# Who issues the stores of the up stage in a hybrid recurrent, attention and expert block on one core

## The chip, the cores and the metric

The kernel runs on one core of a Trainium2 chip. The metric is the device time of one execution in microseconds (us), as the median of several runs.

## The reference

The reference is one layer of a hybrid block over 1024 tokens of width 1024. A gated linear recurrence and a forgetting attention come first; neither is touched here. Behind them stands PEER: every token has 128 experts (8 heads of 16) out of 16384, each with one row of `u_tab` and one of `v_tab`. It is this part that the change is in:

```python
def block(args):
    xb, eb, gb = args
    pre = jnp.einsum('td,tkd->tk', xb.astype(jnp.float32), u_tab[eb].astype(jnp.float32))
    act = jax.nn.gelu(pre) * gb
    return jnp.einsum('tk,tkd->td', act, v_tab[eb].astype(jnp.float32))
```

`experts` (eb) come from two top-16 lists over 128 keys each, and `gates` (gb) are a softmax over the 16 picked scores of each head.

## The kernel before

The program is a row of stages, each a block in which the five engines run their own instruction lists and meet only through semaphores. The stages are: projection, recurrence, attention, output mix, scoring, `experts_up`, `experts_down`, and the last norm. The change is in `experts_up`, the up stage.

The up stage treats the tokens in two ways. The last 640 tokens are dense: for them `gelu(h @ u)` is computed for all 16384 experts, in NK = 128 chunks of 128 experts. The first 384 tokens go by rows: for each of the 384 slots (128 picks of 3 tiles) GpSimd gathers one u row for each of 128 tokens (`fetch`, an indirect DMA of 512 KB into a ring of 6 tiles `u_rows`), and VectorE forms the dot products (`dot`).

One dense chunk c goes through these steps. SyncE loads `u_chunk` (512 KB, two buffers) by `load(c)`. ScalarE copies it to `uT_hi` (`high`, L1559). VectorE subtracts to `uT_lo` (`low`, L1709; for the first 24 chunks GpSimd does it, L1612). TensorE multiplies 48 times into `expert_pre` (L1523), in two halves of 320 tokens, over four PSUM buffers. ScalarE applies the gelu into `expert_acts` (L1573, two buffers). SyncE stores `expert_acts` to `acts_dram` (320 KB, L1493).

Beside this the gates of the dense tokens are spread over the experts, in 160 groups of four tokens. VectorE makes one-hot rows (L1719, L1720), ScalarE multiplies them by the gates (`gate`, L1581 and L1584, eight small instructions for a group), TensorE multiplies them into `spread_ps` (L1513, L1515), and ScalarE copies the result into `pick_memory` (`spread_out`, L1566). When 8 groups are there, a part of 2 MB is stored to `gates_dram` (L1499); there are 20 such stores, one for about five chunks.

All engines walk a common numbering of quarters q, four for a chunk (QUARTERS = 512), and each engine's list is in the order of q. `high(c + 1)` stands at the start of chunk c, the two gelus at its second and fourth quarter. The order within SyncE's list is written out by hand: `load(c + 2)`, which waits for `low(c)`, then a wait for both gelus of chunk c and the store of them, then the gates store that may be due. A wait holds up everything behind it on the engine.

The semaphores that matter: `act_done` counts gelus, `act_stored` and `spread_stored` count stores landed (a gelu waits for the first before it writes a buffer again, `spread_out` for the second), `u_in` counts loads landed.

Of the kernel before, what the change touches and what calls it, by code (L numbers as in the profile page):

```python
# [1377 lines left out]
def experts_up(nc, d, m, sem):  # L1378
# [12 lines left out]
    GROUP, SLOTS, PART = 4, 4, 8  # L1391
# [4 lines left out]
    QUARTERS = 4 * NK  # L1396
# [6 lines left out]
    def paced(q, total, first, stop):  # L1403

        return min(max((q - first) * total // (stop - first), 0), total)

    groups_at = lambda q: range(paced(q, ALL, SPREAD_FROM, SPREAD_TO), paced(q + 1, ALL, SPREAD_FROM, SPREAD_TO))
# [22 lines left out]
    with ExitStack() as own_memory:  # L1430
# [5 lines left out]
        act_out = sb("expert_acts", [P, 2, DENSE])  # L1436
# [3 lines left out]
        spread = m.pick_memory[:, 0:2 * NK * 32].rearrange("p (b e t) -> p b e t", b=2, t=32)  # L1440
# [16 lines left out]
        pre_done, act_done = sem("pre_done"), sem("expert_act_done")  # L1457
        act_stored = [sem("act_stored0"), sem("act_stored1")]
        hot_done, gates_hot = sem("hot_done"), sem("gates_hot")
        spread_done, spread_read = sem("spread_done"), sem("spread_read")  # L1460
        spread_stored = [sem("spread_stored0"), sem("spread_stored1")]
# [10 lines left out]
        def wait_low(engine, c):  # L1472

            if c < POOL_LOWS:
                engine.wait_ge(ulo_pool, c + 1)
            else:
                engine.wait_ge(ulo_dve, c - POOL_LOWS + 1)

        with nc.Block() as block:
            @block.sync  # L1480
            def _(sp):
                def load(c):
                    if c >= 2:
                        wait_low(sp, c - 2)
                    sp.dma_start(u[:, c % 2], d.peer_u_turned[c]).then_inc(u_in[c % 2], 16)

                load(0)
                load(1)
                for c in range(NK):
                    if c + 2 < NK:  # L1490
                        load(c + 2)
                    sp.wait_ge(act_done, 2 * c + 2)
                    sp.dma_start(d.acts[c], act_out[:, c % 2]).then_inc(act_stored[c % 2], 16)  # L1493
                    for q in range(4 * c, 4 * c + 4):
                        for g in groups_at(q):
                            if (g + 1) % PART == 0:
                                part = g // PART
                                sp.wait_ge(spread_read, g + 1)
                                sp.dma_start(d.gates[part].rearrange("p e t -> p (e t)"),  # L1499
                                             spread[:, part % 2].rearrange("p e t -> p (e t)")  # L1500
                                             ).then_inc(spread_stored[part % 2], 16)
                for b in range(2):
                    sp.wait_ge(act_stored[b], 16 * (NK // 2))
                    sp.wait_ge(spread_stored[b], 16 * (ALL // PART // 2))
# [46 lines left out]
            @block.scalar  # L1551
            def _(act):
                A = nc.scalar.activation

                def high(c):
                    act.wait_ge(u_in[c % 2], 16 * (c // 2 + 1))
                    if c >= 2:
                        act.wait_ge(pre_done, 2 * c - 2)
                    A(uhi[:, c % 2], u[:, c % 2], ACT.Copy).then_inc(uhi_done, 1)  # L1559

                def spread_out(g):
                    part, col = divmod(g, PART)
                    act.wait_ge(spread_done, g + 1)
                    if col == 0 and part >= 2:
                        act.wait_ge(spread_stored[part % 2], 16 * (part // 2))
                    A(spread[:, part % 2, :, col * GROUP:(col + 1) * GROUP].rearrange("p e t -> p t e"),  # L1566
                      spread_ps[:, g % 2], ACT.Copy).then_inc(spread_read, 1)

                def gelu(c, half):
                    act.wait_ge(pre_done, 2 * c + half + 1)  # L1570
                    if half == 0 and c >= 2:
                        act.wait_ge(act_stored[c % 2], 16 * (c // 2))
                    A(act_out[:, c % 2, half * WIDTH:(half + 1) * WIDTH], pre[:, (2 * c + half) % 4, 0:WIDTH],  # L1573
                      ACT.Gelu_apprx_tanh).then_inc(act_done, 1)

                high(0)
                def gate(g):
                    t, first = g // GROUPS, g % GROUPS * GROUP
                    act.wait_ge(hot_done, g + 1)
                    for j in range(GROUP):  # L1580
                        A(second_lo[:, g % SLOTS, j], second_hi[:, g % SLOTS, j].bitcast(F32), ACT.Identity,  # L1581
                          scale=gate_lo[:, t % 2, first + j:first + j + 1])
                    for j in range(GROUP):
                        last = A(second_hi[:, g % SLOTS, j], second_hi[:, g % SLOTS, j].bitcast(F32), ACT.Identity,  # L1584
                                 scale=gate_hi[:, t % 2, first + j:first + j + 1].bitcast(F32))
                    last.then_inc(gates_hot, 1)

                for q in range(QUARTERS):
                    c = q // 4
                    if q % 4 == 0 and c + 1 < NK:  # L1590
                        high(c + 1)
                    if q % 2 == 1:
                        gelu(c, q % 4 // 2)
                    for g in groups_at(q):
                        spread_out(g)
                    for g in gates_at(q):
                        gate(g)
                    if q == KEYS_FROM - 4:
                        act.wait_ge(shifted, 1)
                        A(m.pair_val[:], below_top, ACT.Exp).then_inc(exp_done, 1)  # L1600
                    for f in range(F):
                        if q == min(dots_end[f] + 2, QUARTERS - 1):
                            act.wait_ge(dot_done, P * (f + 1))
                            A(dots[:, f], dots[:, f], ACT.Gelu_apprx_tanh).then_inc(dots_read, 1)

            @block.gpsimd
            def _(pool):
# [377 lines left out]
def hybrid_block(nc, args, stop=None):  # L1985
# [22 lines left out]
    with ExitStack() as memory:  # L2008
# [90 lines left out]
        with h2, picks:  # L2099
            with h2_rows_part:  # L2100
                score(nc, d, m, sem)
            if stop == "score": return m
            experts_up(nc, d, m, sem)
# [36 lines left out]
```

## Time and profile before

| What | Value |
|---|---|
| Runs | 2991.67, 2984.30, 2984.37 us; median 2984.37 |
| Profiled execution, first to last instruction (span) | 2987.8 us |
| Up stage, dense chunks | from 889.7 to 1988 us in the span |
| TensorE busy over the span | 2742.9 us (92%) |
| VectorE, ScalarE, GpSimd busy | 2346.0, 1253.3, 1435.8 us |
| Moved by DMA | 754.28 MB, mean 252 GB/s |

The profile gives no time of its own for what lies around the span. The span is 3.4 us over the median of the runs.

The profile names the engines PE (TensorE matmul), PEld (its weight load), DVE (VectorE), ACT (ScalarE), POOL (GpSimd) and SP (SyncE); SPq and ACTq are DMA issues on the queue of that engine. A row of a group names line, engine, operation and `out<-in` by the program's tile names. "Idle before" is the time for which the engine sat idle ahead of the instruction, and the arrow names what it waited for.

### The profile page before, as it was taken

Reading aid. Unit: us, or ns where it says so; the run is one execution under the profiler, and the core shown is the slowest. Engines: PE = TensorE matmul, PEld = TensorE weight load, DVE = VectorE, ACT = ScalarE, POOL = GpSimd, SP = SyncE. Lnnn points to the kernel's source line nnn. Section 1 sums busy time; section 2 is a strip of 40 time slices with the busy share of each in tenths; the row PEclk is TensorE's granted clock in tenths of the full one; section 3 lists DMA queues with packets and bytes.
Section 4 is the critical chain, followed back from the end, with each engine's and each line's share of the span. In section 5 each row is a group of like instructions: output and inputs, shape, how many; then the busy total and the mean of one; then the engine's idle time right before and its main releaser. Section 6 shows DMA issues by size and latency. Waiting matters only on the chain. (4 is left out here: it accounts for less than half of the span.)

```text
span 2987.8 us, 40185 instructions
## 1 busy us (share of the span) xinstructions
PE 2742.9 (92%) x15003; PEld 2397.9 (80%) x15003; DVE 2346.0 (79%) x4170; ACT 1253.3 (42%) x2507; POOL 1435.8 (48%) x1107
## 2 busy tenths in 40 slices
PE   7998799989989999999999999954999999999996
PEld 6776576459989999999999999953887787787875
DVE  3375786327968888997898988747999999999997
ACT  3244333112223277777778788722222222222222
POOL 1111210004745765555455555534666666667663
PEclk9999799989999999999999999986999999999998
DMA  4110100211103799999899999989999999999996
GB/s 117 36 42 14 57 1 22 84 58 42 37 29 119 268 330 328 355 346 326 325 355 347 339 370 362 356 314 344 375 382 362 380 383 366 382 383 372 385 375 226
DMA packets 315442, 754.28 MB, mean 252 GB/s; under 512 B 22944, under 2 KB 141728, under 8 KB 312688
## 3 DMA queue, kind: packets, MB, share of 16 engines
q0 software_dynamic: 111104, 403.02, 36.4%
q1 hardware_dynamic: 203088, 344.50, 32.6%
q10 hardware_dynamic: 1056, 4.19, 0.3%
q8 instruction: 119, 1.95, 0.3%
q14 instruction: 75, 0.61, 0.1%
HBM read 659.35 MB, written 92.27 MB: 252 GB/s over the span
## 5 line engine op out<-in xcount | busy, mean ns | idle before, releaser
L1829 POOL DMA_INDIRECT v_rows<-in_peer_v,row_numbers x384 | 614.6, 1601 | 370.8 <-DVE y L1893 242.1
L1621 POOL DMA_INDIRECT u_rows<-in_peer_u,row_numbers x384 | 535.7, 1395 | 421.1 <-DVE row_weights L1726 367.5
L1523 PE MATMUL expert_pre<-h2T,uT_hi 128*128 128x320 f32 x4096 | 674.4, 313 | 43.7 <-DVE uT_lo L1709 27.6
L1523 PEld LDWEIGHTS expert_pre<-h2T,uT_hi 128*128 128x128 f32 x4096 | 614.7, 190 | 51.5 <-DVE uT_lo L1709 32.7
L1935 PE MATMUL expert_out<-v_hi,w_hi 128*128 128x512 f32 x1280 | 503.5, 393 | 91.1 <-DVE w_lo L1872 91.0
L1893 DVE SCALAR_TENSOR_TENSOR y<-v_rows,row_weights,y 128x1024 f32<-128x1024 f32 x384 | 489.1, 1282 | 62.6 <-DMA v_rows<-in_peer_v,row_numbers 45.5
L1935 PE MATMUL expert_out<-v_lo,w_hi 128*128 128x512 f32 x1280 | 501.5, 392 | 0.0
L1935 PE MATMUL expert_out<-v_hi,w_lo 128*128 128x512 f32 x1280 | 500.9, 391 | 0.0
L1726 DVE CUSTOM_DVE_ANT_0 u_rows<-u_rows,h_rows_kept 128x1024 f32<-128x1024 f32 x384 | 468.8, 1248 | 17.2 <-DMA u_rows<-in_peer_u,row_numbers 17.2
L1935 PEld LDWEIGHTS expert_out<-v_hi,w_hi 128*128 128x128 f32 x1280 | 242.1, 189 | 149.7 <-DVE w_lo L1872 99.6
L1853 ACT ACTIVATE w_hi<-acts_times_gates 128x640 fp32r<-128x640 f32 x128 | 94.8, 741 | 626.9 <-DVE acts_times_gates L1865 626.9
L1523 PE MATMUL expert_pre<-h2T,uT_lo 128*128 128x320 f32 x2048 | 343.5, 309 | 0.0
L1523 PEld LDWEIGHTS expert_pre<-h2T,uT_lo 128*128 128x128 f32 x2048 | 313.3, 189 | 0.0
L1935 PEld LDWEIGHTS expert_out<-v_hi,w_lo 128*128 128x128 f32 x1280 | 242.3, 189 | 50.9
L1935 PEld LDWEIGHTS expert_out<-v_lo,w_hi 128*128 128x128 f32 x1280 | 242.0, 189 | 49.9
L1581 ACT ACTIVATE second_hot_lo<-second_hot_hi,gateT_lo 128x128 fp32r<-128x128 f32 x640 | 203.5, 393 | 64.3 <-DVE second_hot_hi L1720 64.1
L1709 DVE TENSOR_TENSOR uT_lo<-u_chunk,uT_hi 128x1024 fp32r<-128x1024 f32 x104 | 127.2, 1223 | 123.6 <-ACT uT_hi L1559 122.7
L1584 ACT ACTIVATE second_hot_hi<-second_hot_hi,gateT_hi 128x128 fp32r<-128x128 f32 x640 | 203.4, 392 | 0.0
L1566 ACT ACTIVATE pick_memory<-spread_ps 128x512 f32<-128x512 f32 x160 | 178.8, 1118 | 18.1 <-PE spread_ps L1515 18.0
L1573 ACT ACTIVATE expert_acts<-expert_pre 128x320 f32<-128x320 f32 x256 | 112.4, 439 | 161.6 <-PE expert_pre L1523 160.9
L1559 ACT ACTIVATE uT_hi<-u_chunk 128x1024 fp32r<-128x1024 f32 x128 | 135.6, 1060 | 101.6 <-DMA u_chunk<-in_peer_u_turned 101.6
L1851 ACT ACTIVATE v_hi<-v_chunk 128x1024 fp32r<-128x1024 f32 x128 | 134.5, 1051 | 95.7 <-PE expert_out L1935 78.0
(300 smaller groups left out, 4188.8 us busy)
## 6 DMA issues: line engine op xcount, KB each, us to landing
u_chunk<-in_peer_u_turned SPq DMA_DIRECT2D x128, 512.0 KB, 6.9
v_chunk<-in_peer_v SPq DMA_DIRECT2D x128, 512.0 KB, 9.6
acts_dram<-expert_acts SPq DMA_DIRECT2D x128, 320.0 KB, 4.9
gates_dram<-pick_memory SPq DMA_DIRECT2D x20, 2048.0 KB, 11.0
acts_times_gates<-acts_dram SPq DMA_DIRECT2D x128, 320.0 KB, 10.5
gates_group<-gates_dram SPq DMA_DIRECT2D x32, 1280.0 KB, 18.5
w_in_columns<-in_w_in SPq DMA_DIRECT2D x20, 512.0 KB, 4.0
wq_tile<-in_peer_wq SPq DMA_DIRECT2D x16, 512.0 KB, 4.0
```

What stands on the lines that cost most here:

```text
L1523: last = nc.tensor.matmul(pre[:, (2 * c + half) % 4, 0:WIDTH], part[:, c % 2, k], m.h2T[:, t, k, HALVES[half]], start=n == 0, stop=n == le ...
L1559: A(uhi[:, c % 2], u[:, c % 2], ACT.Copy).then_inc(uhi_done, 1)
L1566: A(spread[:, part % 2, :, col * GROUP:(col + 1) * GROUP].rearrange("p e t -> p t e"), spread_ps[:, g % 2], ACT.Copy).then_inc(spread_read, 1)
L1581: A(second_lo[:, g % SLOTS, j], second_hi[:, g % SLOTS, j].bitcast(F32), ACT.Identity, scale=gate_lo[:, t % 2, first + j:first + j + 1])
L1584: last = A(second_hi[:, g % SLOTS, j], second_hi[:, g % SLOTS, j].bitcast(F32), ACT.Identity, scale=gate_hi[:, t % 2, first + j:first + j ...
L1621: pool.indirect_dma_start(rows[:, k % RING], None, d.peer_u, bass.IndirectOffsetOnAxis(ap=m.row_of[:, f, slot:slot + 1], axis=0)).then_inc ...
L1709: v.tensor_tensor(ulo[:, c % 2], u[:, c % 2], uhi[:, c % 2].bitcast(F32), ALU.subtract).then_inc(ulo_dve, 1)
L1726: v.tensor_tensor_reduce(out=rows[:, k % RING], in0=rows[:, k % RING], in1=m.h2_kept[:, f], scale=1.0, scalar=0.0, op0=ALU.mult, op1=ALU.a ...
L1829: pool.indirect_dma_start(rows[:, k % ROW_RING], None, d.peer_v, bass.IndirectOffsetOnAxis(ap=m.row_of[:, f, slot:slot + 1], axis=0)).then ...
L1851: nc.scalar.activation(vhi[:, n % 2, c], vt[:, x % V_RING], ACT.Copy).then_inc(vhi_done, 1)
L1893: v.scalar_tensor_tensor(out=m.y[:, f], in0=rows[:, k % ROW_RING], scalar=m.row_weight[:, f, slot:slot + 1], in1=m.y[:, f], op0=ALU.mult, ...
L1935: last = nc.tensor.matmul(out[:, bank], a[:, n % 2, c, tokens], e[:, n % 2, c, cols], start=opens and k == 0, stop=closes and k == len(ter ...
```

## The change

ScalarE now issues the stores of activations and gates in the up stage; SyncE's list keeps the loads of u, and at its end the waits for the last stores. `store_acts(c - 1)` stands behind `high(c + 1)` at the start of chunk c, `store_gates` at the start of the quarter that follows the spreading of a part's last group. The data moved and the semaphores are the same.

```diff
                 for c in range(NK):
                     if c + 2 < NK:
                         load(c + 2)
-                    sp.wait_ge(act_done, 2 * c + 2)
-                    sp.dma_start(d.acts[c], act_out[:, c % 2]).then_inc(act_stored[c % 2], 16)
-                    for q in range(4 * c, 4 * c + 4):
-                        for g in groups_at(q):
-                            if (g + 1) % PART == 0:
-                                part = g // PART
-                                sp.wait_ge(spread_read, g + 1)
-                                sp.dma_start(d.gates[part].rearrange("p e t -> p (e t)"),
-                                             spread[:, part % 2].rearrange("p e t -> p (e t)")
-                                             ).then_inc(spread_stored[part % 2], 16)
...
+                def store_acts(c):
+                    act.wait_ge(act_done, 2 * c + 2)
+                    act.dma_start(d.acts[c], act_out[:, c % 2]).then_inc(act_stored[c % 2], 16)
+
+                def store_gates(part):
+                    act.wait_ge(spread_read, PART * (part + 1))
+                    act.dma_start(d.gates[part].rearrange("p e t -> p (e t)"),
+                                  spread[:, part % 2].rearrange("p e t -> p (e t)")
+                                  ).then_inc(spread_stored[part % 2], 16)
+
                 for q in range(QUARTERS):
                     c = q // 4
                     if q % 4 == 0 and c + 1 < NK:
                         high(c + 1)
+                    if q % 4 == 0 and c:
+                        store_acts(c - 1)
+                    for g in groups_at(q - 1) if q else []:
+                        if (g + 1) % PART == 0:
+                            store_gates(g // PART)
                     if q % 2 == 1:
                         gelu(c, q % 4 // 2)
...
+                    if q == QUARTERS - 1:
+                        store_acts(c)
```

In the lists below, names in square brackets are the semaphores that an instruction waits for. This is SyncE's list before the change, around the first gates store, with the load that follows it:

```order
L1485 DMA u_chunk<-in_peer_u_turned 128x1024 [waits u_lo_by_dve]
L1493 DMA acts_dram<-expert_acts 128x640 [waits expert_act_done]
L1499 DMA gates_dram<-pick_memory 128x4096 [waits spread_read]
L1485 DMA u_chunk<-in_peer_u_turned 128x1024 [waits u_lo_by_dve]
L1493 DMA acts_dram<-expert_acts 128x640 [waits expert_act_done]
```

And this is the whole of SyncE's list of the up stage with the change, up to the branch that ends the stage:

```order
L1480 UNCONDITIONAL_BRANCH [waits barrier_Pool_Activation_PE_DVE_SP_release]
L1485 DMA u_chunk<-in_peer_u_turned 128x1024 x2
L1485 DMA u_chunk<-in_peer_u_turned 128x1024 [waits u_lo_by_pool] x24
L1485 DMA u_chunk<-in_peer_u_turned 128x1024 [waits u_lo_by_dve] x102
L1479 UNCONDITIONAL_BRANCH [waits act_stored1,spread_stored1,spread_stored0,act_stored0]
```

Each load now waits for a subtraction alone; no store and no wait for a gelu stands between two loads.

ScalarE's list before, at the place in the program that corresponds to the first gates store:

```order
L1584 ACTIVATE second_hot_hi<-second_hot_hi,gateT_hi 128x128 x4
L1559 ACTIVATE uT_hi<-u_chunk 128x1024 [waits pre_done,u_in1]
L1566 ACTIVATE pick_memory<-spread_ps 128x4x128 [waits spread_done]
L1573 ACTIVATE expert_acts<-expert_pre 128x320 [waits act_stored0,pre_done]
L1581 ACTIVATE second_hot_lo<-second_hot_hi,gateT_lo 128x128 [waits hot_done]
```

The same place with the change, where a line of ScalarE has a number lower by ten:

```order
L1574 ACTIVATE second_hot_hi<-second_hot_hi,gateT_hi 128x128 x4
L1549 ACTIVATE uT_hi<-u_chunk 128x1024 [waits pre_done,u_in1]
L1580 DMA acts_dram<-expert_acts 128x640 [waits expert_act_done]
L1556 ACTIVATE pick_memory<-spread_ps 128x4x128 [waits spread_done]
L1584 DMA gates_dram<-pick_memory 128x4096 [waits spread_read]
L1563 ACTIVATE expert_acts<-expert_pre 128x320 [waits act_stored0,pre_done]
L1571 ACTIVATE second_hot_lo<-second_hot_hi,gateT_lo 128x128 [waits hot_done]
```

ScalarE has 148 DMA issues more, 128 of activations and 20 of gates. The store of activations stands right behind the copy to `uT_hi`; 15 of the 20 gates stores stand right behind a `spread_out`, the other five behind a store of activations.

## Rows read from the trace of the kernel before

**Rows 1.** The page: busy time of each engine over the span.

```profile
PE 2742.9 (92%) x15003; PEld 2397.9 (80%) x15003; DVE 2346.0 (79%) x4170; ACT 1253.3 (42%) x2507; POOL 1435.8 (48%) x1107
```

**Rows 2.** Stretches: length, busy us of PE, PEld, DVE, ACT, POOL, granted clock, DMA share, GB/s.

```profile
998.00:1063.00 65.00, 58.70 (x392) 56.86 (x393) 49.58 (x69) 23.35 (x52) 57.80 (x36) 1.00 0.91 321
1063.00:1988.00 925.00, 896.88 (x6329) 891.08 (x6327) 793.13 (x1187) 703.12 (x1730) 491.01 (x354) 0.99 0.92 343
1736.00:1871.00 135.00, 134.58 (x964) 134.28 (x964) 112.80 (x178) 110.34 (x273) 77.18 (x56) 1.00 0.96 364
```

**Rows 3.** Who waited for whom, 1063 to 1988 us: total us, times, longest.

```profile
DVE uT_lo L1709 <- ACT uT_hi L1559: 122.7, 40, 8.2
ACT uT_hi L1559 <- DMA u_chunk<-in_peer_u_turned: 97.1, 23, 7.4
ACT second_hot_lo L1581 <- DVE second_hot_hi L1720: 64.1, 45, 3.4
ACT expert_acts L1573 <- PE expert_pre L1523: 42.0, 43, 3.1
PE expert_pre L1523 <- DVE uT_lo L1709: 27.6, 21, 4.0
DVE u_rows L1726 <- DMA u_rows<-in_peer_u,row_numbers: 1.8, 2, 1.0
```

**Rows 4.** The same stretch, waits of SyncE's queue.

```profile
SPq L1493 <- ACT expert_acts L1573: 813.6, 105, 15.6
```

**Rows 5.** Timeline of SyncE's queue, ScalarE and VectorE from 1734 us: start, duration, instruction.

```profile
1738.09 1.23 DVE L1709 TENSOR_TENSOR uT_lo<-u_chunk,uT_hi 128x1024 fp32r<-128x1024 f32 x1 [1.36 <-ACT uT_hi L1559]
1743.72 0.43 SPq L1499 DMA_DIRECT2D gates_dram<-pick_memory  x1
1744.20 0.47 SPq L1485 DMA_DIRECT2D u_chunk<-in_peer_u_turned  x1
1757.48 1.06 ACT L1559 ACTIVATE uT_hi<-u_chunk 128x1024 fp32r<-128x1024 f32 x1 [4.01 <-DMA u_chunk<-in_peer_u_turned]
```

**Rows 6.** Timeline of TensorE: four of its 21 waits for `uT_lo`, first and last among them.

```profile
1163.94 4.63 PE L1523 MATMUL expert_pre<-h2T,uT_hi 128*128 128x320 f32 x16 [4.00 <-DVE uT_lo L1709]
1342.05 3.43 PE L1523 MATMUL expert_pre<-h2T,uT_hi 128*128 128x320 f32 x16 [2.62 <-DVE uT_lo L1709]
1577.31 2.03 PE L1523 MATMUL expert_pre<-h2T,uT_hi 128*128 128x320 f32 x12 [2.14 <-DVE uT_lo L1709]
1973.17 2.62 PE L1523 MATMUL expert_pre<-h2T,uT_hi 128*128 128x320 f32 x16 [3.17 <-DVE uT_lo L1709]
```

**Rows 7.** Stretches behind four of TensorE's waits, columns as in Rows 2.

```profile
1161.50:1172.00 10.50, 8.06 (x39) 8.06 (x39) 9.34 (x15) 9.15 (x23) 3.62 (x3) 0.67 0.76 274
1342.00:1347.00 5.00, 4.95 (x23) 4.96 (x24) 5.00 (x9) 5.00 (x14) 2.39 (x2) 0.66 0.85 262
1396.00:1401.00 5.00, 4.12 (x19) 4.13 (x20) 5.00 (x8) 5.00 (x16) 1.56 (x2) 0.72 0.33 60
1486.00:1491.00 5.00, 4.75 (x22) 4.76 (x23) 5.00 (x7) 1.59 (x6) 0.00 (x0) 0.66 0.35 143
```

**Rows 8.** DMA issues over the whole span: engine, count, KB each, median us to landing.

```profile
u_chunk<-in_peer_u_turned SPq DMA_DIRECT2D x128, 512.0 KB, 6.9
gates_dram<-pick_memory SPq DMA_DIRECT2D x20, 2048.0 KB, 11.0
u_rows<-in_peer_u,row_numbers POOLq DMA_INDIRECT x384, 7.3
```

**Rows 9.** Issues: ns min/median/max, first and last start; last row as in Rows 5.

```profile
L1485 SPq DMA_DIRECT2D u_chunk<-in_peer_u_turned x128: 327/433/2738, 882.2 to 1963.8; - x128
L1493 SPq DMA_DIRECT2D acts_dram<-expert_acts x128: 319/320/327, 899.0 to 1988.0; - x128
L1621 POOL DMA_INDIRECT u_rows<-in_peer_u,row_numbers x384: 932/1440/3046, 988.3 to 1966.1; - x192
1991.24 0.51 ACTq L1845 DMA_DIRECT2D y<-x_dram  x1
```

## The prediction

> **What bounds the kernel now.** I read the page first [rows 1]: TensorE is busy 92% of the span, no other engine over 79%, so time comes out of the kernel only where TensorE waits or runs at a low clock. Then the stretches of the stage that the change touches [rows 2]. The first 23 chunks end by about 1063 us. In the last part of them, from 998, TensorE idles 6.3 us while GpSimd, which does the subtractions there, is busy 57.8 of 65 us; no store is in that chain, and I expect nothing from it. The long stretch is 1063 to 1988 us, with 105 of the 128 chunks: 896.9 busy of 925, so 28.1 us idle.
>
> What would the stretch take if TensorE never waited? Between 1736 and 1871 us it is busy for 134.6 of 135 us at clock 1.00 and does 964 matmuls, 7.14 in a us. The 6329 matmuls of the long stretch take 886 us at that pace, 39 less than 925. That is the most that any change of the waits in this stretch can give: 28 us of idleness and some 10 in which it ran slower than full pace.
>
> The waits [rows 3] say what the idle time is: 27.6 us in 21 waits for `uT_lo` of VectorE. VectorE in turn waits 122.7 us for `uT_hi` of ScalarE, and ScalarE 97.1 us in 23 waits for the DMA of `u_chunk`. So a late load is the head of the chain. The timeline shows how one becomes late [rows 5]. At 1743.72 SyncE issues a gates store of 2 MB and at 1744.20, behind it in the same queue, a load of u. ScalarE gets the load only at 1757.48, 13.3 us after its issue, having sat idle for 4.0 us. The median load takes 6.9 us and a gates store 11.0 [rows 8].
>
> Why is the load behind the store at all? It reuses the buffer of a chunk whose `uT_lo` was finished at 1738.09 + 1.23 = 1739.3, so it could have gone 4.9 us earlier. SyncE was held by the wait for the gelus: that wait comes 105 times and takes 813.6 us, 7.7 us of every chunk [rows 4].
>
> **The change, part by part.**
>
> Loads without the stores in front. Each load is now issued when its subtraction is done, some 4 to 5 us sooner, in the example 4.4 us before the gates store instead of 0.5 us behind it. The next one goes during the store, but from another queue. A load needs 6.9 us typically, and the one in the example would have been wanted at 1753.5 (1757.48 less the 4.01 of idleness), 14.2 us after 1739.3: even the 13.3 us that it took behind the store would do. The longest of ScalarE's waits is 7.4 us; with a landing as slow as now and 4.9 us of lead, 2.5 would be left of it, and nothing of those under 4.9. I take the 97.1 us to fall below 10.
>
> What of that reaches TensorE. I followed each of its 21 waits back in the timeline; four of them are shown [rows 6]. Ten come directly behind a wait of ScalarE for the load: 19.9 us together, the first 4.00 and the last 3.17. Four more, 1.9 us, come in the one to four chunks after such a wait, while VectorE works off what piled up. The other seven, 5.8 us, have a VectorE that is late by its own work, like the 2.14 at 1577; these stay. So 21.8 us go.
>
> The clock. Behind four of the ten waits the granted clock is 0.67, 0.66, 0.72 and 0.66 [rows 7], a mix of its two levels 2.4 and 1.2 GHz; ahead of each TensorE had idled for 2.5 to 4 us. The cost is the missing share times the length: 3.5 + 1.7 + 1.4 + 1.7 = 8.3 us. It goes with the waits that it follows.
>
> 148 issues on ScalarE. On SyncE an issue takes 0.32 us for activations and 0.43 for gates; one on ScalarE's queue, in the next stage, 0.51 [rows 9]. In the long stretch that is 105 x 0.32 + 20 x 0.43 = 42 us more on ScalarE, 64 at 0.51 each. What can't overlap is a gates store: in 15 of 20 cases it waits for the `spread_out` just ahead to end, and ScalarE stands still for an issue. Its cover is the one to two chunks of lead with which `high` runs ahead of TensorE. I charge 5 us of new waits of TensorE; the bounds are 0 and the 42 us if no cover held.
>
> Longer reuse of buffers. A store of activations is issued behind `high(c + 1)`, some 2 to 3 us later than now, and can stand in the same queue behind a gates store of 11 us. The gelu that waits for it comes about one and a quarter chunks later, 11 us. A few gelus may wait a us or two; TensorE needs their PSUM buffer only two chunks on. Costed at nothing, inside the 5 us.
>
> Contention. The long stretch moves 343 GB/s x 925 us = 317 MB; in 886 us that is 358 GB/s. The stretch at full pace has 364 with the DMA engines 0.96 busy [rows 2]: near the edge, but it was run with TensorE never waiting. The gathers are a third party with 512 KB each, 384 of them in 978 us [rows 9], one in 2.55 us or 206 GB/s. While load, gates and gathers all run, a third of 364 GB/s would leave them 121, for the 4.3 us that a load takes at that rate: they fall behind by 0.37 MB, or 1.8 us. The ring of six tiles gives 6 x 2.55 = 15.3 us against a landing of 7.3 [rows 8], and VectorE waited only 1.8 us for gathers in the whole stretch [rows 3]. Costed at nothing.
>
> A rule of the Trainium skill speaks against the change: by its page "DMA: Bandwidth & Descriptors", section "Issuing engines are not separate DMA queues", transfers started by different engines run on the same 16 DMA engines and interleave, and several issuers save only issue time. By that rule alone the new queue itself brings nothing, and the rows do not dispute it; the gain would then be that of the earlier issue alone, which by the row of 4.9 us is nearly all of it.
>
> Sum: 21.8 + 8.3 - 5 = 25 us. The profiled span becomes 2987.8 - 25 = 2963; the span stands 3.4 us over the median run, so the median goes from 2984.4 to 2959.
>
> **The rivals.**
>
> The DMA engines are the bound. In that case a queue of its own only rearranges who waits: loads land early, and gates, activations or gathers late by as much. For it: the DMA share is 0.92 over the stretch and 0.96 at full pace. Against it: the 364 GB/s above. VectorE's `dot` would wait for gathers behind each of the 20 gates stores, 1.8 us each, 36 in all; if 21 of these reach TensorE by way of `uT_lo`, 4 us of gain are left: 2980.
>
> Half a gain. The stalls of ScalarE vanish, but VectorE, busy 793 of 925 us, or ScalarE, at full pace with its new issues at (110.3 + 6) of 135, take their place: 5.8 us of TensorE's waits are already of this kind. If they triple, that is 11.6 us more where I charged 5, and if half of the clock's 8.3 stays too, 11 of the 25 are lost: 2970.
>
> Slower, by ScalarE as an issuer. A DMA issue can be held up: on SyncE the longest took 2.74 us [rows 9]. On ScalarE everything stands behind it: `high`, then `uT_lo`, then TensorE. What is freed is 97 us; over 125 stores it is used up at 0.78 us each. From there ScalarE is busier than now, and at 1.6 us each it holds 703 + 200 = 903 us of work, over the 886 that TensorE needs; with a third of its remaining waits for VectorE and TensorE (64.1 + 42.0, so 35) it takes 938 us: 13 us slower, 2997. Against it: medians of 0.32 and 0.43, and a median is what counts over 125 of them.
>
> No effect at all would need that the load isn't held by SyncE's wait; the 813.6 us and the 4.9 us of the example exclude it.
>
> **How the numbers follow.** A measurement of this kernel tells a change from none at about 0.3%, 9 us, so faster is below 2975.4 and slower above 2993.3. My forecast, 2959, has 0.65, with its own range of 2950 (nothing charged to ScalarE, and 4 of the seven other waits' 5.8 us gone too) to 2969 (15 us charged). Half a gain has 0.15, most of it still faster; the DMA bound 0.12; the slower case 0.08. Faster is 0.65 + 0.12 = 0.77, same 0.15, slower 0.08. The range of 8 in 10 goes from 2949 to 2980: above it lie the slower case and half of the DMA case.
>
> **What would show it.** In the changed kernel's profile ScalarE's waits for `u_chunk` should be under 10 us, SyncE's queue should wait for `uT_lo` in every chunk, TensorE's waits for `uT_lo` of VectorE should be near 10 us instead of 27.6, the granted clock should be 1.00 in the stretch, and the up stage should end near 1963. The issues on ScalarE should last 0.3 to 0.5 us. I am wrong if `u_rows` appears as what VectorE waits for, if the landing of gathers rises over 10 us, if ScalarE's waits for its gates stores appear, or if the last stage takes the time back.

## The result: 2947.5 us, faster by 1.3%, just outside the range

The changed kernel takes 2947.52 us (median of 4 runs, 2946.64 to 2948.64). The kernel before, now with 4 runs, has a median of 2988.02 us (2984.30 to 2997.29); the fourth run, 2997.29, moved it up from the 2984.4 that the forecast started from. The ratio is 0.9869, with a 95% interval of 0.9844 to 0.9894. The prediction was 2959 us with a range from 2949 to 2980. The direction was right, and the gain is larger than forecast: 36.9 us below 2984.4, where 25 were forecast.

The page of the profile after, first line of busy times, answers to [rows 1]. The span is 2944.8 us against 2987.8.

```profile
PE 2728.3 (93%) x15003; PEld 2387.4 (81%) x15003; DVE 2348.3 (80%) x4170; ACT 1262.6 (43%) x2507; POOL 1431.7 (49%) x1107
```

To compare the up stage between kernels I measure it from the first matmul of `expert_pre` to the start of the last gelu, and split it where VectorE does its first `uT_lo` (chunk 24). The views by stretch give both parts: first the kernel before, then the changed one. Columns are as in [rows 2].

```profile
889.70:1067.80 178.10, 170.82 (x1146) 168.72 (x1147) 147.79 (x470) 58.13 (x109) 125.22 (x93) 0.99 0.60 203
1067.80:1987.60 919.80, 892.09 (x6295) 886.28 (x6293) 789.21 (x1183) 698.58 (x1721) 486.76 (x351) 0.99 0.92 344
```

```profile
890.20:1065.70 175.50, 171.94 (x1158) 170.63 (x1159) 146.64 (x462) 59.19 (x112) 121.05 (x94) 0.99 0.60 209
1065.70:1947.10 881.40, 878.65 (x6283) 877.02 (x6282) 790.63 (x1185) 706.38 (x1718) 487.92 (x351) 1.00 0.95 358
```

The later part shrank from 919.8 to 881.4 us, by 38.4. TensorE idled 27.7 us in it and now idles 2.75, and it is busy for 878.7 instead of 892.1 us. The two parts don't hold quite the same work: 12 matmuls more fall into the earlier part of the changed kernel (1158 against 1146) and 12 fewer into the later one, 1.7 us at the 7.14 matmuls in a us of the stretch at full pace. The earlier part gave 2.6 us, and what follows the up stage 2.5 (1000.2 to 997.7). With the start 0.5 us later, that is the 43.0 us between the two spans.

Who waited for whom in the later part of the changed kernel, beside [rows 3]:

```profile
ACT expert_acts L1563 <- PE expert_pre L1513: 73.1, 73, 3.1
DVE uT_lo L1716 <- ACT uT_hi L1549: 63.4, 35, 4.6
DVE u_rows L1733 <- DMA u_rows<-in_peer_u,row_numbers: 20.6, 18, 4.1
ACT expert_acts L1563 <- DMA acts_dram<-expert_acts: 3.7, 2, 2.7
PE expert_pre L1513 <- DVE uT_lo L1716: 2.7, 4, 2.1
```

ScalarE's wait for `u_chunk`, 97.1 us before, isn't in the list any more. TensorE's waits for VectorE went from 27.6 us in 21 to 2.7 in 4, where near 10 us had been forecast, and the stage ends at 1947 instead of the forecast 1963. VectorE's waits for gathers rose from 1.8 us to 20.6; the prediction had named this as a sign of being wrong.

SyncE's queue in the same stretch, beside [rows 4]: it now waits for the subtraction with each of its 102 loads, and for nothing else.

```profile
SPq L1485 <- DVE uT_lo L1716: 825.8, 102, 11.9
```

The timeline around one gates store shows the new order, beside [rows 5]: the subtraction ends at 1437.08 + 1.23 = 1438.31, the load is issued at 1438.34, and the gates store follows at 1438.84 on ScalarE's queue. The load landed 9.3 us later; the row of 1453.54, in which ScalarE takes it, has no wait.

```profile
1437.08 1.23 DVE L1716 TENSOR_TENSOR uT_lo<-u_chunk,uT_hi 128x1024 fp32r<-128x1024 f32 x1 [4.12 <-ACT uT_hi L1549]
1438.34 0.33 SPq L1485 DMA_DIRECT2D u_chunk<-in_peer_u_turned  x1
1438.84 0.33 ACTq L1584 DMA_DIRECT2D gates_dram<-pick_memory  x1
1444.55 0.33 ACTq L1580 DMA_DIRECT2D acts_dram<-expert_acts  x1
1453.54 1.04 ACT L1549 ACTIVATE uT_hi<-u_chunk 128x1024 fp32r<-128x1024 f32 x1
```

### The profile page after: what moved, and what is told of

Same layout as the page of the kernel before. It is cut to its first block and busy times, and to the rows that moved or that the text cites. A ratio compares the mean times of both kernels' runs of the same rounds, so it can differ in the third digit from the quotient of the medians.

```text
span 2944.8 us, 40185 instructions
## 1 busy us (share of the span) xinstructions
PE 2728.3 (93%) x15003; PEld 2387.4 (81%) x15003; DVE 2348.3 (80%) x4170; ACT 1262.6 (43%) x2507; POOL 1431.7 (49%) x1107
## 5 line engine op out<-in xcount | busy, mean ns | idle before, releaser
L1513 PE MATMUL expert_pre<-h2T,uT_hi 128*128 128x320 f32 x4096 | 667.3, 311 | 16.1 <-POOL uT_lo L1619 13.3
L1716 DVE TENSOR_TENSOR uT_lo<-u_chunk,uT_hi 128x1024 fp32r<-128x1024 f32 x104 | 127.2, 1223 | 64.2 <-ACT uT_hi L1549 63.4
L94 PE MATMUL product<-hT_hi_lo,w_in_hi 128*128 128x512 f32 x640 | 156.2, 396 | 3.4 <-DVE hT_hi_lo L223 2.4
```

Source lines behind the costliest of these rows:

```text
L94: last = nc.tensor.matmul(to, w[:, i % 2, k], m.hh[:, part, k, cols], start=n == 0, stop=n == len(terms) - 1)
L1513: last = nc.tensor.matmul(pre[:, (2 * c + half) % 4, 0:WIDTH], part[:, c % 2, k], m.h2T[:, t, k, HALVES[half]], start=n == 0, stop=n == le ...
L1716: v.tensor_tensor(ulo[:, c % 2], u[:, c % 2], uhi[:, c % 2].bitcast(F32), ALU.subtract).then_inc(ulo_dve, 1)
```

## The experiments

The change does two things to a load: it frees it from the wait for the gelus, and it takes the stores out of its queue. It also moves two kinds of stores and adds 148 issues to ScalarE. The first four kernels separate these.

**Stores on ScalarE, loads as late as before.** The changed kernel with one line more on SyncE:

```diff
                     if c + 2 < NK:
                         load(c + 2)
+                    sp.wait_ge(act_done, 2 * c + 2)
```

> The stores go on ScalarE's queue as in the change, but SyncE still waits for both gelus of chunk c before the next load, so the loads are issued as late as before the change. Theory A (the 2 MB gates store ahead of a load in the same queue makes that load late, and either a queue of its own or an earlier issue cures it): nearly the whole gain stays, 2950 to 2960 us, ScalarE waits under 25 us for u_chunk instead of 97. Rival B (the hold of 7.7 us a chunk is what costs): the gain is gone, 2980 to 2988 us. Rival C (the 16 DMA engines are shared, so a queue of its own brings nothing by itself): 2980 to 2988 us as well, with loads landing in 13 us behind each gates store.

The median is 2941.88 us, beside 2978.77 for the kernel before on the same chip, which the first four kernels share; the ratio is 0.9881 (0.9845 to 0.9916). The up stage took 1060.8 us. The loads behind the gates stores go nearly as late after their subtraction as before, 4.0 us by the median (4.9 before). ScalarE waited 19.2 us for `u_chunk`; the longest wait, 4.4, is for the first chunk of all, which every kernel has. In the later part:

```profile
ACT uT_hi L1550 <- DMA u_chunk<-in_peer_u_turned: 14.6, 11, 2.7
PE expert_pre L1514 <- DVE uT_lo L1717: 2.1, 1, 2.1
```

Theory A stands; B, that the hold in every chunk costs, falls. The loads don't land in 13 us either, as C had it. But this kernel changes two things, and not the queue alone. ScalarE issues a gates store sooner than SyncE did, so that the next load follows it by 0.8 to 7.4 us, 3.9 by the median; before, all 20 followed by 0.4 to 0.6 us. What the queue alone does is best seen where a load still goes close behind the store. In three profiles with all stores on ScalarE landing times can be read: the changed kernel's two and the last one of this section. There ten loads are issued 0.2 to 1.0 us behind a gates store, and they landed in 9.9 to 11.7 us. In the kernel before the 20 loads behind a gates store landed in 11.5 to 15.5, 13.4 by the median. So another queue, without the store of activations in it too, takes some 2.5 us off such a landing, an estimate from these two groups; at a greater distance the landings are shorter still (in the changed kernel's first profile 7.0 to 9.0 us for the twelve loads 4.5 to 9 us behind a store). How the gain of the stage splits between the two, no run shows.

**Loads early, all stores on SyncE.** Only SyncE's order is changed in the kernel before (`stores` holds its two waits and stores, unchanged):

```diff
                 for c in range(NK):
+                    if c >= 2:
+                        stores(c - 2)
                     if c + 2 < NK:
                         load(c + 2)
-                    sp.wait_ge(act_done, 2 * c + 2)
...
+                stores(NK - 2)
+                stores(NK - 1)
...
```

> All stores stay on SyncE and its queue, and nothing is added on ScalarE; only SyncE's order changes: the stores of chunk c - 2, then the load for c + 2, so that a load waits for its subtraction alone and goes some 4 us earlier, still behind the gates store in the queue. Theory A: a load of 13.3 us fits into the 14.2 us that it then has, so 2948 to 2955 us, as the change. Rival D (a queue of its own is what matters): 2975 to 2988 us, ScalarE still waits for the load behind each gates store.

The median is 2949.89 us, the ratio 0.9898 (0.9855 to 0.9940). The up stage took 1061.5 us, and ScalarE waited 4.5 us for `u_chunk`, in 2 waits, both for the first two chunks. In the later part TensorE's waits are gone too:

```profile
PE expert_pre L1529 <- DVE uT_lo L1715: 2.3, 2, 2.1
```

D falls: with the loads early a queue of their own isn't needed, and nor is ScalarE. Here too the new order moves the load away from the store: it follows 1.9 to 8.2 us behind it.

**Only the gates stores on ScalarE.** The kernel before without the gates stores on SyncE, and with `store_gates` of the change on ScalarE.

```diff
                     sp.dma_start(d.acts[c], act_out[:, c % 2]).then_inc(act_stored[c % 2], 16)
-                    for q in range(4 * c, 4 * c + 4):
...
+                    for g in groups_at(q - 1) if q else []:
+                        if (g + 1) % PART == 0:
+                            store_gates(g // PART)
...
```

> Only the 20 gates stores go to ScalarE; the stores of activations stay on SyncE, with the wait for the gelus between the loads. Theory A: 2950 to 2960 us, as with both moved but the loads late. Rival B (the hold in every chunk costs): 2980 to 2988 us.

The median is 2947.82 us, the ratio 0.9885 (0.9844 to 0.9925). The up stage took 1062.2 us. So 20 of the 148 moved stores are enough. The next load follows a gates store by 1.2 to 7.8 us here.

**Only the stores of activations on ScalarE.** The other half of the change:

```diff
                     if c + 2 < NK:
                         load(c + 2)
-                    sp.wait_ge(act_done, 2 * c + 2)
-                    sp.dma_start(d.acts[c], act_out[:, c % 2]).then_inc(act_stored[c % 2], 16)
...
+                    if q % 4 == 0 and c:
+                        store_acts(c - 1)
...
```

> Only the 128 stores of activations go to ScalarE; the gates stores stay on SyncE between the loads, each behind its wait for spread_out. In four of five chunks a load is free to go early, in the fifth it stands behind the gates store, late as before. Theory A: the late loads are exactly these, so hardly any gain, 2975 to 2988 us. Rival B: four fifths of the gain, 2955 us.

The median is 2949.53 us, the ratio 0.9916 (0.9883 to 0.9948). The up stage took 1071.1 us: 27 of the 41 us are won (21 of 34 by the second profile of the kernel before, see below), where I expected hardly any. Here theory A, in the form that I had given it, was wrong. These are the waits for the load and of TensorE in its later part, first in this kernel, then in the one with only the gates moved:

```profile
ACT uT_hi L1557 <- DMA u_chunk<-in_peer_u_turned: 38.4, 12, 8.0
PE expert_pre L1521 <- DVE uT_lo L1715: 9.2, 7, 3.8
```

```profile
ACT uT_hi L1551 <- DMA u_chunk<-in_peer_u_turned: 37.2, 20, 4.5
PE expert_pre L1515 <- DVE uT_lo L1710: 3.5, 7, 2.1
```

ScalarE waits for as long in both, 38 and 37 us, but TensorE loses 9.2 us in one and 3.5 in the other, and the later parts take 893.2 and 884.4 us. About 2 us of TensorE's waits, at chunk 80, are VectorE's own lateness in both; this wait stands in eleven of the twelve profiles. The rest differs by the long waits. Over the whole up stage the kernel before had ten waits of ScalarE over 5 us (7.38 the longest) and fifteen below; this one has two over 5 (8.02 and 6.09), and the one with the gates moved has none. In this kernel TensorE waits 3.83 us right behind the 8.02, and 2.10 right behind one of 4.76, but only 0.36 behind the 6.09.

In the two profiles of the kernel before, hardly any wait of ScalarE under 4 us is followed by one of TensorE within 4 us (one, by 0.36). The six between 4.0 and 4.9 behind the first chunk are followed by 0.42 to 2.31 us, or by nothing in one case, and those over 5 by anything from nothing to 4.0. So a single wait of up to 4 us costs TensorE next to nothing; above that the cost differs from chunk to chunk, and the length of the wait alone doesn't give it.

18 of the 20 loads are still issued 0.4 us behind a gates store here. But the loads behind a gates store go 0 to 5.4 us after their subtraction, 2.2 by the median, where it was 0.8 to 7.5 and 4.9 before, and that fits the fewer long waits. This is the nearest that the runs come to an earlier issue by itself.

**A swap on SyncE alone.** The kernel before, with a due gates store behind the next load instead of ahead of it; the loads still wait for the gelus.

```diff
+                load(2)
                 for c in range(NK):
-                    if c + 2 < NK:
-                        load(c + 2)
                     sp.wait_ge(act_done, 2 * c + 2)
                     sp.dma_start(d.acts[c], act_out[:, c % 2]).then_inc(act_stored[c % 2], 16)
+                    if c + 3 < NK:
+                        load(c + 3)
                     for q in range(4 * c, 4 * c + 4):
```

> The kernel before with one swap on SyncE: when a gates store is due, the next load is issued ahead of it instead of behind it. All stores stay on SyncE, and the loads still wait for the gelus. If only the load directly behind the 2 MB is too late, ScalarE's waits for u_chunk stay under 4.5 us each, and the up stage takes 1060 to 1064 us. If the next load, about 8 us later in the same queue, is as late, 1080 to 1098 us.

One run of 2953.55 us, beside 2982.72 of the kernel before on the same chip. The up stage took 1060.8 us, the same as with the stores on ScalarE and late loads. Its later part:

```profile
ACT uT_hi L1560 <- DMA u_chunk<-in_peer_u_turned: 25.0, 19, 3.4
PE expert_pre L1524 <- DVE uT_lo L1710: 2.1, 3, 1.7
```

The load that comes behind the store now follows it by 5.5 to 11.1 us. So the loss was in 20 places where a load stood right behind 2 MB in one queue, and the three cures of it are equally good, 1060.8 to 1061.5 us. The changed kernel is 3 to 5 us below them, about half of it in the earlier part. What they have in common is that no load is issued within 0.6 us behind a gates store in its own queue.

**What an issue costs ScalarE.** More issues behind `store_acts`, three or six in each chunk, of 8 KB each:

```diff
                 def store_acts(c):
                     act.wait_ge(act_done, 2 * c + 2)
+                    for j in range(3):
+                        act.dma_start(d.extra[c, j], m.ident[0:16]).then_inc(act_stored[c % 2], 16)
                     act.dma_start(d.acts[c], act_out[:, c % 2]).then_inc(act_stored[c % 2], 16)
```

> The changed kernel with three more DMA issues on ScalarE in each chunk (8 KB each, a constant into scratch memory, so nearly no bytes). An issue takes 0.33 us, so in the 105 later chunks this is 104 us more of ScalarE, which was idle for 175 of 881 us there, 41 of which its stores' issues took already. Theory A (the idle time of ScalarE covers issues): the up stage stays within 10 us of 1057. Rival E (each issue holds up the chain through high): 1160 us.

> The same with six more issues in each chunk, 208 us in the 105 later chunks, more than the 134 us that ScalarE has left. Theory A: the cover is used up, ScalarE becomes the bound and the up stage grows by at least 74 us, to 1131 or more. If issues run beside activations and cost ScalarE nothing, it stays at 1057. Rival E: 1265 us.

With three more the up stage took 1057.6 us, the same as the change. With six more it took 1108.9 us, 52 more than the change, and the one run 2997.42 us, slower than the kernel before with 2982.72 and 2978.38 in its runs on this chip. That is less than the bound of 74 that I gave. The extra issues, in the kernel with six:

```profile
L1581 ACTq DMA_DIRECT2D extra_dram<-ident x768: 308/442/1972, 896.8 to 1998.3; - x192
```

And its later part by stretch:

```profile
1063.70:1995.60 931.90, 901.14 (x6295) 889.90 (x6293) 791.45 (x1183) 695.53 (x1721) 475.01 (x351) 0.99 0.95 345
```

750 issues start on ScalarE in it. They last 393 us together, more than 0.44 us each, as many are longer than the median. Taken one by one from the timeline, 209 of the 393 us lie within an activation. The bound had left that out. In the changed kernel it is 35 of 40 us in 124 issues, and with three more in each chunk 167 of 225. Its waits show the way in which it reaches TensorE:

```profile
DVE uT_lo L1718 <- ACT uT_hi L1549: 107.9, 48, 7.0
ACT second_hot_lo L1571 <- issue: 68.9, 35, 6.9
...
PE spread_ps L1503 <- ACT second_hot_hi L1574: 16.7, 14, 4.8
```

The gates rows for the spreading are late, 16.7 us of TensorE, and `high` is too, by which VectorE waits 107.9 us where it was 63.4; of TensorE that is 10.7 us over the whole stage. So the way through `high`, which rival E named, is open here, but only once ScalarE is full. The cover is there, and it ends somewhere between four and seven issues a chunk; the change uses one, and a second in every fifth chunk.

**What repeats.** The kernel before and the changed one once more.

> The kernel before, unchanged, profiled a second time, to see what repeats. The up stage (first matmul of expert_pre to last gelu) took 1097.9 us in the first profile and 1056.9 with the change; I expect 1097 to 1099 again, with 25 to 30 us of TensorE's waits for uT_lo, while what follows the up stage, 1000.2 us before and 997.7 with the change, moves by several us without a cause in the program.

> The changed kernel, unchanged, profiled and timed a second time. The up stage should repeat at 1057 us within 2, TensorE's waits for VectorE's uT_lo under 4 us, and the ratio to the kernel before be 0.984 to 0.990.

The kernel before had an up stage of 1092.1 us (1097.9 in its first profile), 22.8 us of TensorE's waits for VectorE, and 997.7 us behind the stage. Both of the first two are below what I expected. The changed kernel had 1057.7 us (1056.9), 1.9 us of such waits, and the ratio 0.9878 (0.9849 to 0.9907): 2942.82 us, against 2979.55 for the kernel before on that chip. The gain repeats, though in the stage it is 34.4 us in this pair of profiles and 41.0 in the first: the kernel before varies by 5.8 us there, the changed one by 0.8. Over all twelve profiles the stage starts at 881.9 to 891.8 us, and what follows it takes from 984.0 to 1003.8, without any order in either. This is why whole times differ by 10 us where the stage of the changed kernel agrees within 1.

**The remaining waits.** The changed kernel with GpSimd's share of the subtractions cut:

```diff
-    POOL_LOWS = 24
+    POOL_LOWS = 14
```

> The changed kernel with GpSimd doing the subtraction for the first 14 chunks instead of 24, VectorE from there on. TensorE's last waits of any size in the up stage, 3.4 us in four, are for GpSimd, whose subtraction stands behind gathers from chunk 13 on; in the later chunks it is at full pace. If these four waits are all that is left, the up stage goes from 1056.9 to 1053 or 1054 us, which the time of the whole kernel can't tell from no change. Rival: VectorE, which does the key steps of the first tiles there, is late instead, 1057 to 1065 us.

The ratio is 0.9884 (0.9851 to 0.9916) and the up stage 1058.3 us. The waits for GpSimd after the first are gone, but those for VectorE rose to 6.2 us, 4.2 of it in chunk 14, where it takes over:

```profile
PE expert_pre L1513 <- DVE uT_lo L1716: 6.2, 3, 4.2
```

Nothing is gained; the changed kernel is not beaten by this one.

## Why the prediction was right in kind and too small in size

**Right: what bounded the stage, and the chain.** The head of the chain was the late load, and the late load was the one right behind the gates store. The eight profiles in which behind the first chunk no load makes ScalarE wait over 5 us, and ScalarE isn't overloaded, have an up stage of 1056.9 to 1062.2 us; the kernel before has 1092.1 and 1097.9. The forecast that ScalarE's waits for `u_chunk` fall below 10 us holds (5.4 us, all of it for the first two chunks), and so does the granted clock of 1.00.

**Right in the result, open in the share: the earlier issue.** The prediction set the rule of the Trainium skill's "DMA: Bandwidth & Descriptors", section "Issuing engines are not separate DMA queues", against the row of 4.9 us, and found that the earlier issue gives nearly all. Loads early in the same queue gave 1061.5 us. But stores on ScalarE with late loads gave 1060.8, 31 or 37 us less than the kernel before, by which of its profiles one takes. How much of that comes from the greater distance between store and load is open. By the rule several issuers save only issue time. The measurement differs: close behind a gates store a load landed in 9.9 to 11.7 us from another queue, and in 11.5 to 15.5 from the same. The same page's section "Queues, rings and completion order", by which each DMA engine takes turns between the queues that have work for it, agrees with this.

**Wrong: the sum.** The step that failed is "Sum: 21.8 + 8.3 - 5 = 25 us"; in the later part it was 38.4. All three of its terms were off in the same direction; counted for the same work, the 5 us charged for ScalarE are the largest error:

- The waits that go, 21.8 us: TensorE's waits for VectorE fell by 24.9 us in the stage's later part (27.6 to 2.7). I had kept seven waits, 5.8 us, as VectorE's own lateness. Only the one of 2.14 at 1577, in chunk 80, with a small one just ahead of it, has a counterpart (2.13 us in the changed kernel). The others were gone in every cured kernel, where 1.9 to 3.5 us remain in all, so I take them for late effects of the stalls. (The kernel with GpSimd's share cut has 6.2, but 4.2 of it in chunk 14, the first that VectorE takes over.) I had followed a stall for four chunks and stopped. In the second pair of profiles these waits fell by 20.9 us (22.8 to 1.9), so this term was off by no more than the kernel before varies.
- The slower pace, 8.3 us: TensorE's busy time in the later part fell by 13.4 us, 1.7 of it by the 12 matmuls fewer, so by 11.7 for the same work. In the second pair it fell by 11.8 (891.0 to 879.2), with 2 matmuls fewer. I had counted the four stretches in which the granted clock was seen low, and left out what was spread elsewhere. The first estimate, by the stretch at full pace, had 10.5, and 39 for both together; the measured 38.4 nearly reaches that ceiling. Where the 3.4 us beyond the 8.3 were lost isn't settled.
- The 5 us charged for ScalarE: nothing was lost. The 124 issues of the later part lasted 40 us, and 35 of these passed while an activation ran. One issue and even four a chunk are covered.

Beside the sum, 2.6 us came from the earlier part, where I expected nothing, or 4.3 with its 12 matmuls more. The changed kernel has 175.5 and 176.6 us there in its two profiles and 175.3 with three more issues a chunk; the kernel before has 178.1 and 178.0, and the first five experiments 177.8 to 178.9. What makes this is left open. The 2.5 us behind the stage are within its scatter.

**The rivals.** "The DMA engines are the bound" was half true and harmless: VectorE's waits for gathers rose to 20.6 us, and their landing from 7.3 us to 7.8 by the median, but neither reached TensorE; the stretch ran at 358 GB/s with a DMA share of 0.95, which is the 358 worked out. "Half a gain" didn't occur. "Slower, by ScalarE as an issuer" does exist, at six issues a chunk more, and its point is much further off than the 0.78 us a store that was given: four issues of 0.44 by the median, 1.8 us in a chunk, cost nothing.

**The range.** Its lower end, 2949, lies 1 us below the case with nothing charged to ScalarE and 4 us of the seven waits gone too. That case kept the clock's 8.3 us; the ceiling of 39 us from the same section would have put it at 2945. The median measured lies 1.5 us below the range.

## What to carry to other kernels

Look at what stands directly ahead of a double-buffered load in its queue: a rare large store costs little by itself, but the load behind it lands in 13 us instead of 7, and swapping the two, issuing the load earlier, or issuing the store on another engine are equally good cures. The cheapest was the swap of two issues on one engine. When a stretch at full pace lies in the same stage, work out what the stage would take at that pace: here the ceiling of 39 us was nearer to the measured gain, 38.4 us in the first pair of profiles and 33.0 in the second, than the sum over single waits, 25. Most of the waits that looked independent went with the stalls. And a stall costs only what it is over the slack: 20 waits of ScalarE of up to 4.5 us left TensorE with 3.5 us of waiting, 2.1 of it VectorE's own. Of the ten over 5 us eight were followed within 3 us by 19.1.

## What the runs showed of the chip

- An issue on SyncE's queue takes 0.33 us when it stands alone and 0.43 when it follows another at once: the loads have a median of 0.328 us in the changed kernel and 0.433 in the one before, and the longest 0.43 against 2.74 us. On ScalarE a store of activations took 0.326 us by the median, and 0.445 behind three others, up to 1.77.
- ScalarE's sequencer issues transfers while an activation runs: 35 of 40 us of issues did in the later part of the changed kernel, and 209 of 393 us in the kernel with six more.
- A load of 512 KB issued 0.4 to 0.6 us behind a store of 2 MB in the same queue landed in 11.5 to 15.5 us (20 loads); issued 0.2 to 1.0 us behind it from another queue, in 9.9 to 11.7 (10 loads). The median of all loads is 6.9 and 6.7 us.
- What follows the up stage took from 984 to 1004 us in twelve profiles although its program is the same in all, and what stands ahead of it from 882 to 892; nothing here explains that.
